# One sum per token for the norms, a block transposition on VectorE, and other partition halves in the first level of a triangular inverse

## The reference, cut to what matters

```python
def rmsnorm(x, g):
    y = xf * lax.rsqrt(jnp.mean(xf * xf, axis=-1, keepdims=True) + EPS)
    return (y * g.astype(jnp.float32)).astype(x.dtype)
```

```python
kb = k * beta[..., None]
Lmat = jnp.where(strict, jnp.einsum('bhnid,bhnjd->bhnij', kb, k) * decay, 0.0)
rhs = jnp.concatenate([v * beta[..., None], kb * jnp.exp(gc)[..., None]], axis=-1)
sol = lax.linalg.triangular_solve(eye + Lmat, rhs, left_side=True, lower=True, unit_diagonal=True)
```

## Time and profile before

| what | value |
|---|---|
| median of 3 runs | 1916.28 us (1915.13 to 1918.05) |
| the profiled execution, its own time | 1917.52 us |
| its span, first to last instruction | 1915.6 us |
| PE busy | 99% of the span |
| DVE, ACT, POOL busy | 62%, 41%, 16% |
| chain that ended last | PE 91%, DVE 5%, ACT 2%, issue 1%, POOL 1% |
| mean granted TensorE clock | 0.994 |

### The profile page before, as it was taken

How to read it: one execution, slowest core, us unless ns; L and a number is a source line. 1 busy time by engine, 2 the same in 40 slices (tenths; PEclk the granted TensorE clock), 3 DMA queues, 4 the chain that set the end, 5 groups by cost and what they waited for, 6 DMA issues and landing times.

```text
span 1915.6 us, 29959 instructions
## 1 busy us (share of the span) xinstructions
PE 1889.2 (99%) x10740; PEld 1539.3 (80%) x10740; DVE 1195.6 (62%) x1844; ACT 792.1 (41%) x1495; POOL 301.1 (16%) x222
## 2 busy tenths in 40 slices
PE   9999999999999999999999999999999999999997
PEld 7888878888888767777778888888887888888886
DVE  4997554333333777777745856737778568476474
ACT  4234443232233555555533423424547534243242
POOL 2532222111011200000111100101221211011012
PEclk9999999999999999999999999999999999999998
DMA  5232323232322112111112332232311123323231
GB/s 195 90 101 98 133 70 109 95 99 89 108 88 99 45 56 68 55 62 62 51 45 88 110 110 88 88 109 89 122 66 56 67 88 110 100 88 99 88 109 66
DMA packets 46946, 170.49 MB, mean 89 GB/s; under 512 B 5344, under 2 KB 5504, under 8 KB 46720
## 3 DMA queue, kind: packets, MB, share of 16 engines
q1 hardware_dynamic: 45648, 165.12, 26.0%
q10 hardware_dynamic: 1200, 3.95, 0.6%
HBM read 166.94 MB, written 2.11 MB: 88 GB/s over the span
## 4 chain that ended last, share of the span: by engine, by line
PE 91%; DVE 5%; ACT 2%; issue 1%; POOL 1%; DMA 0%; DVEq 0%; SPq 0%; POOLq 0%
PE ps L275 19%; PE ps L277 17%; PE ps L276 17%; PE ps L263 9%; PE ps L264 9%; PE ps L265 9%; PE ps L694 1%; PE ps L714 1%; PE ps L669 1%; PE ps L314 1%; DVE scr L1556 1%; DVE scr L1547 1%; DVE Y L1547 1%; PE ps L447 0%; PE ps L315 0%
## 5 line engine op out<-in xcount | busy, mean ns | idle before, releaser
L222 ACT ACTIVATE w_hi<-w_raw 128x1024 fp32r<-128x1024 f32 x304 | 316.9, 1050 | 269.7 <-PE ps L277 176.5
L227 DVE TENSOR_TENSOR w_lo<-w_raw,w_hi 128x1024 fp32r<-128x1024 f32 x255 | 344.4, 1354 | 124.3 <-ACT w_hi L222 123.6
L275 PE MATMUL ps<-A_hi,w_hi 128*128 128x512 f32 x896 | 367.0, 410 | 2.1 <-DVE Y L1046 1.1
L277 PE MATMUL ps<-A_hi,w_lo 128*128 128x512 f32 x896 | 350.6, 391 | 0.0
L276 PE MATMUL ps<-A_lo,w_hi 128*128 128x512 f32 x896 | 350.0, 391 | 0.0
L275 PE MATMUL ps<-B_hi,w_hi 128*128 128x512 f32 x688 | 271.3, 394 | 1.3 <-DVE B_lo L1083 0.9
L277 PE MATMUL ps<-B_hi,w_lo 128*128 128x512 f32 x688 | 268.0, 390 | 0.0
L276 PE MATMUL ps<-B_lo,w_hi 128*128 128x512 f32 x688 | 267.8, 389 | 0.0
L275 PEld LDWEIGHTS ps<-A_hi,w_hi 128*128 128x128 f32 x896 | 168.6, 188 | 39.1 <-issue 2.6
L277 PEld LDWEIGHTS ps<-A_hi,w_lo 128*128 128x128 f32 x896 | 168.6, 188 | 36.5
L276 PEld LDWEIGHTS ps<-A_lo,w_hi 128*128 128x128 f32 x896 | 169.0, 189 | 29.0
(11 more groups left out here) (296 smaller groups left out, 2611.7 us busy)
## 6 DMA issues: line engine op xcount, KB each, us to landing
w_raw<-d_ws SPq DMA_DIRECT2D x304, 512.0 KB, 3.5
X<-d_xT SPq DMA_DIRECT2D x4, 512.0 KB, 7.1
X<-d_xT ACTq DMA_DIRECT2D x1, 2048.0 KB, 8.1
d_out<-X SPq DMA_DIRECT2D x4, 512.0 KB, 2.6
scr<-gc_rows ACTq DMA_DIRECT2D x7, 256.0 KB, 3.2
cst<-d_cst SPq DMA_DIRECT2D x1, 800.0 KB, 11.6
par<-d_par SPq DMA_DIRECT2D x1, 344.5 KB, 3.1
scr<-d_pw SPq DMA_DIRECT2D x1, 256.0 KB, 12.7
```

The source lines that it names most:

```text
L222: nc.scalar.activation(w_hi[:, c], raw[:, c], ACT.Copy).then_inc(S(f"w_hi{s}"), 1)
L227: nc.vector.tensor_tensor(w_lo[:, c], raw[:, c], w_hi[:, c].bitcast(F32), ALU.subtract)\
L275: pe.matmul(ps[bank][:], w_hi[:, c], hi, start=k == 0, stop=False)
L277: last = pe.matmul(ps[bank][:], w_lo[:, c], hi, start=False, stop=k == total - 1)
```

## The change

It has three parts.

1. **The opening.** The sum of the squares moves from POOL to DVE and takes all eight tiles; PE takes one group of token sums. The first two slots of weights are split in halves of 512 columns, with a semaphore for each, and PE's order starts with the half that is there. ACT squares a pair of tiles one step later. `keep_warm` has 19 products in place of 22.
2. **The other token sums.** Except for post0, post1 and fin, POOL adds the last square too and PE takes one group of four matmuls. In `open_late` it stands after the third unit.
3. **The heads.** DVE transposes `TTC` in blocks of 32 x 32 (level 0 has nothing outside 2 x 2 blocks). The level-0 matrices of c = 2, 3 are written to the other half of the partitions, and level 1 becomes a crossed level like 2 to 5, with no transposition on PE and no copy on ACT. Six blocks run ahead of it in one piece.

```diff
@@ the opening, PE
-                if q < 3:
+                if q < 2:
+                    pe.wait_ge(S("early_hi"), count("early_hi", q + 1))
+                    pe.wait_ge(S("early_lo"), count("early_lo", q + 1))
+                    part_blocks(pe, open_bank(q, spare), q, pair, 0, 2 * q + 2, KT, wait)
+                elif q == 2:
                     open_segment(pe, r, q, pair, 0, 2 * q + 2, wait, spare)
-            sums_early(pe, tag, KT, 2)
-            sums_last(pe, tag, KT, 2, FIRST_SQ[KT - 1])
-            open_segment(pe, r, 3, pair, 0, KT - 2, wait, spare)
+            token_sums(pe, tag, KT, 2)
+            open_segment(pe, r, 3, pair, 0, KT - 4, wait, spare)
             pe.wait_ge(S("cst_in"), count("cst_in", 16))
             open_row(pe, tag)
-            open_segment(pe, r, 3, pair, KT - 2, KT, wait, spare)
+            open_segment(pe, r, 3, pair, KT - 4, KT, wait, spare)
...
@@ the opening, DVE in place of POOL
-        def first_sum_squares(pool):
-            pool.wait_ge(S("w_lo3"), count("w_lo3", 1))
-            for m in range(1, KT - 1):
...
+        def first_sum_squares(dve):
+
+            for m in range(1, KT):
+                dve.wait_ge(S("n0_sq"), count("n0_sq", m + 1))
                 if m > 1:
-                    pool.wait_ge(S("n0_ss"), count("n0_ss", m - 1))
-                nc.gpsimd.tensor_tensor(SS[:], FIRST_SQ[0] if m == 1 else SS[:], FIRST_SQ[m], ALU.add)\
+                    dve.wait_ge(S("n0_ss"), count("n0_ss", m - 1))
+                nc.vector.tensor_tensor(SS[:], FIRST_SQ[0] if m == 1 else SS[:], FIRST_SQ[m], ALU.add)\
                     .then_inc(S("n0_ss"), 1)
@@ the token sums
-            for m in range(1, n - 1):
+            for m in range(1, n - (tag in POST)):
                 pool.wait_ge(S(tag + "_sq"), count(tag + "_sq", m + 1))
...
         def token_sums(pe, tag, n, bank):
-            sums_early(pe, tag, n, bank)
-            sums_last(pe, tag, n, bank)
+
+            pe.wait_ge(S(tag + "_ss"), count(tag + "_ss", n - 1))
+            for c in range(NCH):
+                last = pe.matmul(ps[bank][:, c:c + 1], SS[:, c * P:(c + 1) * P], ones[:, 0:1],
+                                 start=c == 0, stop=c == NCH - 1)
+            last.then_inc(S(tag + "_sum"), 1)
@@ open_late
             for s in range(3):
                 open_segment(pe, r, s, pair, 0, KT - late, wait, spare)
-                if s == 1:
-                    sums_early(pe, tag, KT, 2)
-                elif s == 2:
-                    sums_last(pe, tag, KT, 2)
+            token_sums(pe, tag, KT, 2)
@@ delta_pe
-            dense(4, 3)
+            dense(6, 4)
             pe.wait_ge(S("zeros"), count("zeros", ZEROS))
-            for i in range(2):
-                pe.wait_ge(S("d_tt"), at("d_tt", i + 1))
-                for c in (2 * i, 2 * i + 1):
-                    last = transposed64(pe, ps[4 - i], TTC, c)
-                last.then_inc(S("d_ptr"), 1)
-            dense(2, 1)
...
@@ delta_dve
-                        v.tensor_tensor(x[half_], LAv[half_, 2 * i:2 * i + 2, 0, half_],
+                        v.tensor_tensor(x[half_of(b ^ i)], LAv[half_, 2 * i:2 * i + 2, 0, half_],
                                         twice(level(0))[half_], ALU.mult).then_inc(S("d_x"), 1)
                     dve.wait_ge(S("d_x"), at("d_x", 2 * i + 2))
                     v.tensor_tensor(two(pair64(TTC, i)), twice(ident64), x, ALU.subtract).then_inc(S("d_tt"), 1)
+                    dve.wait_ge(S("d_tt"), at("d_tt", i + 1))
+                    if i == 0:
+                        v.transpose(pair64(TC, 0), pair64(TTC, 0)).then_inc(S("d_t"), 1)
+                    else:
+                        for b in range(2):
+                            v.transpose(pair64(TC, 1)[half_of(b)], pair64(TTC, 1)[half_of(1 - b)])\
+                                .then_inc(S("d_t"), 1)
```

More of the change, by code:

```diff
@@ L387, in build, with early_half, squares @@
         FIRST_SQ = [tile(SG, 1 + m) for m in range(KT)]
+        def early_half(s, part):
+            return slice(s * 1024 + part * 512, s * 1024 + (part + 1) * 512)
         def first_norm_act(act):
+            def squares(*tiles):
+                for m in tiles:
+                    nc.scalar.activation(FIRST_SQ[m], tile(X, m), ACT.Square).then_inc(S("n0_sq"), 1)
             for q in range(SLOTS):
@@ L677, in delta_pe @@
             last.then_inc(S("d_trv"), 1)
[L678 removed]
+            dense(6, 4)
             pe.wait_ge(S("zeros"), count("zeros", ZEROS))
[L680 to L689 removed]
+            def crossed_level(l):
+                if l > 1:
+                    for i in range(2):
+                        pe.wait_ge(S("d_tt"), at("d_tt", 2 * (l - 1) + i + 1))
+                else:
+                    pe.wait_ge(S("d_t"), at("d_t", 3))
+                    pe.wait_ge(S("d_kvr"), at("d_kvr", 2 * NCH))
                 for n in range(2):
@@ L698, in crossed_level @@
                                 last.then_inc(S("d_px"), 1)
[L699 to L705, removed]
+                if l > 1:
+                    for n in range(2):
+                        for b in range(2):
+                            for i in range(2):
+                                last = pe.matmul(square64(ps[6 + i], n, b ^ i), square64(TC, 2 * i + n, b),
+                                                 ident64[64 * b:64 * b + 64, :], start=True, stop=True)
+                                if n and b:
+                                    last.then_inc(S("d_ttr"), 1)
                 fill(l, 0)
@@ L723, in delta_pe @@
                 for i in range(2):
[L724 to L729, removed]
-                    for c in (2 * i, 2 * i + 1):
[L731 to L738, removed]
+                    pe.wait_ge(S("d_tt"), at("d_tt", 2 * (l - 1) + i + 1))
+                    for c in (2 * i, 2 * i + 1):
+                        last = pe.matmul(square64(ps[4 + i], c % 2, 1), LAv[0:64, c, 0, 64:P],
+                                         square64(TC, c, 0), start=True, stop=True)
                     last.then_inc(S("d_px"), 1)
-                    if l > 1:
-                        for c in (2 * i, 2 * i + 1):
-                            last = transposed64(pe, ps[6 + i], TC, c)
-                        last.then_inc(S("d_ttr"), 1)
+                    for c in (2 * i, 2 * i + 1):
+                        last = transposed64(pe, ps[6 + i], TC, c)
+                    last.then_inc(S("d_ttr"), 1)
                 fill(l, 0)
@@ L746, in delta_pe @@
                     pe.wait_ge(S("d_x"), at("d_x", 2 * l + 3 + i))
-                    if l == 1:
-                        if i:
-                            pe.wait_ge(S("d_kvr"), at("d_kvr", 3 * NCH))
-                        pe.wait_ge(S("d_o1"), at("d_o1", 0))
-                    else:
-                        pe.wait_ge(S("d_ttc"), at("d_ttc", 8 + 2 * (i + 1)))
-                    for c in (2 * i, 2 * i + 1):
-                        if l == 1:
-                            for b in range(2):
-                                last = pe.matmul(columns(square64(ps[6 + i], c % 2, b), l, 0), square64(TTC, c, b),
-                                                 columns(square64(XB, c, b), l, 0), start=True, stop=True)
-                        else:
-                            last = pe.matmul(square64(ps[6 + i], c % 2, 0), square64(XB, 4 + c, 1),
-                                             diagonal(TTF, c, 1), start=True, stop=True)
+                    pe.wait_ge(S("d_ttc"), at("d_ttc", 8 + 2 * (i + 1)))
+                    for c in (2 * i, 2 * i + 1):
+                        last = pe.matmul(square64(ps[6 + i], c % 2, 0), square64(XB, 4 + c, 1),
+                                         diagonal(TTF, c, 1), start=True, stop=True)
                     last.then_inc(S("d_pt"), 1)
@@ L1835, in _ @@
             pe.wait_ge(S("const"), count("const", 2))
-            keep_warm(pe, 22)
+            keep_warm(pe, 19)
             def glu_round(i, first):
@@ L2087, in _ @@
                 v.tensor_scalar(half[:, at:at + n], par_range(name, n), 0.5, None, ALU.mult).then_inc(S("halved"), 1)
-            for m in range(KT):
-                x_loaded(dve, m)
-                norm_lo(dve, "n0", "mix_pre", pairA, m)
-                if m % 2:
-                    split_lo(dve, 0, m // 2)
+            first_low_parts(dve)
+            first_sum_squares(dve)
             token_mean(dve, "n0", 2, D)
```

53 lines of the change are left out of this document (37 added, 16 removed).

## The result

The changed kernel takes 1899.39 us in the median of four runs (1897.6 to 1902.05), the kernel before 1915.7 on the same chip (1914.38 to 1918.05). The ratio is 0.9916 with a 95% interval of 0.9900 to 0.9931: 16.3 us faster. The forecast was 1897.8, in a range of 1894.0 to 1904.0; the saving was put at 18.5.

What follows compares the result with a forecast made beforehand. PE was taken as the bound, busy 1889.2 of 1915.6 us. Gains of 5.2 (opening), 4.1 (token sums), 9.0 (heads) and 0.2 (na and head 0) sum to 18.5, from 1916.28 to 1897.8 us; range 1894.0 to 1904.0.

Steps and rivals of the forecast that it cites:

- The opening: Up to 37.32 us: PE starts earlier and doesn't wait at its token sums, round ends at 32.1; gain 5.2 us.
- the second price: Old opening, 29.5 to 33.1 us: behind an idle PE the clock is 0.53 and ten matmuls take 3.6 us.
- The token sums: Sums after the opening: 0.90 us saved each at nf0, kv, n_f1, 0.9 at n1, 0.5 at ln; gain 4.1.
- the port question: At n1: POOL's addition starts just ahead of DVE's split, which is held on the shared port and late by 1.0 us.
- The third rival: At n1 DVE's split goes first, POOL's addition ends at 286.4 and PE waits 0.9 us: 1898.7 us; chance 0.15.
- The heads: Heads 1 to 7: dropped transposition and crossed level 1 save PE 1.29 us a head, 9.0 in all.
- It fits by a hair: Level 1 in the heads: DVE's mask ends at 755.44 us, PE asks for it at 755.59.
- na and head 0 together: PE gains 0.9 us at na, but DVE sets head 0; gain 0.2, up to 1.1 if DVE's chain comes forward.
- So that wait only grows: Start of head 0: PE's wait of 1.21 us for `TTC` gets longer as PE gains 0.9 at na.
- the five rivals: Chances: dear transpositions 0.12, slower than before 0.02, port at n1 0.15, opening gives less 0.13, later stage takes it back 0.05.
- dear transpositions: In the heads: DVE's transpositions take more than 0.35 us each; at 0.6 the loss is 6.0, 1903.8 us; chance 0.12.

Runs made afterwards that it cites:

- the extra transpositions: The changed kernel with two more 64x128 transpositions on DVE in each head, ahead of level 1: 1903.4 us, ratio to before 0.9942.
- the sum on POOL: The changed kernel with the opening's sum of squares on POOL again, half slots and all else as changed: 1904.03 us, ratio to before 0.9942.
- the whole slots: The changed kernel with the first two slots of weights whole as before, the sum still on DVE: 1900.52 us, ratio to before 0.9925.

## Why the prediction was right, and where it was not

**The opening** was right in its steps: first block at 8.46 (8.4 forecast), sums at 25.06 (25.3), additions of 0.78 (0.74) done at 23.75 (24.2), no wait, upper clock, next round at 31.93 (32.1). The first of the seven additions starts at 18.29, where 19.0 was reckoned, and that makes up for their being a little longer. That the first block varies, from 8.27 to 9.23 over the executions with the half slots, was not in it, nor that the gain does: 4.7 to 5.5 where the sum is on DVE. The two don't go together in every execution: behind the block at 8.27 the gain was 5.1, behind that at 8.46 5.5. And the second price, the 3.6 us at 0.53, is one that the old opening doesn't pay in every execution: with the heads alone changed it didn't, and lay 1.9 ahead.

**The token sums** were right: 0.95 for 0.90 at the three late ones. At ln PE waits 0.25 for POOL. At n1 the port question went as taken: POOL first, the split held. POOL and DVE after:

```profile
277.98 1.33 POOL L466 TENSOR_TENSOR SS<-SS,SQ 128x512 f32<-128x512 f32 x1 [0.80 <-ACT SQ L452]
```

```profile
278.08 2.31 DVE L228 TENSOR_TENSOR w_lo<-w_raw,w_hi 128x1024 fp32r<-128x1024 f32 x1
280.58 0.16 DVE L494 TENSOR_SCALAR tok<-ps 128x4 f32<-128x4 f32 x1 [0.20 <-PE ps L488]
```

A split that takes 1.23 alone takes 2.31 and ends at 280.39, ahead of PE's request at 280.49. The third rival didn't come. POOL's addition ends at 279.31, and 1.23 behind that would be 280.54. The Trainium skill, "SBUF — State Buffer", section "SBUF: two separate sides", has the rule: of a DVE instruction with two inputs in SBUF and a GpSimd instruction that reads SBUF, the one that starts first holds the shared port pair for its whole instruction. The trace agrees to 0.15, with a price of 1.08 here.

**The heads.** 0.31 a transposition for the 0.3 taken; 1.3 a head for 1.29. The Trainium skill, "VectorE: DVE Perf Modes", section "The three transpose paths", gives 311 ns for 128 x 128 in bf16; for fp32 the trace has the same, 0.31 at 744.09. "It fits by a hair" was right in heads 2 to 6 and wrong in head 1, where DVE begins later (its first mask takes 0.70) and PE waits 0.37, and in head 7, where level 2 waits 0.55 for the update where it waited 0.42.

**The failed step** is na and head 0 together, "Gain 0.2". Its times up to the mask were right. Less the 6.75 by which PE is early ahead of na, level 1 was forecast at 667.65 and came at 667.72, the mask's end at 669.35 and came at 669.34. What followed was not: level 2 forecast at 670.65 came at 671.61. I wrote "So that wait only grows" and gave the longer wait no price beyond itself, though I had priced just that in the opening, where a wait of 1.07 was followed by 3.6 us at 0.53. The missing term is 1.0 in one execution and 4.0 in the other (1.7 and 4.7 less the 0.7 that head 0 costs with the wait filled). With the 0.4 of head 1 that is 1.4 in one execution and 4.4 in the other, on either side of the 2.2 by which the measured saving is short of 18.5. That the forecast came so near is luck in part: how long the clock stays down is no part of its sum, and the 19.9 between the two traces hold 2.7 that are low stretches of before.

None of the five rivals was this one. The nearest, dear transpositions, has the right engine and the wrong reason: they are not dear, but head 0 has no cover for them.

## What to carry to other kernels

Work that moves from PE to DVE costs nothing in the rounds where DVE has finished by the time PE asks; look for the one round where DVE sets the time already, since there the work moves onto the path. Where it makes PE stand still for longer, add what the clock can take afterwards, as a range, and consider a few idle products or a smaller edit for that round alone. When two profiled executions are compared, take out first the stretches that differ in granted clock only.

## What the hardware showed that I had not expected

- Behind PE's waits of 2.02 to 2.69 us in head 0 the lower clock came in all six executions that had one (the changed kernel twice, the heads alone, the extra transpositions, the sum on POOL, the whole slots). Behind waits of 1.15 to 1.27 at the same place it came in none of five (before, the opening alone, the sums alone, and the two with level 1 uncrossed there). Behind the wait of 1.07 to 1.08 at 27 us it came in two of three, behind that of 1.00 at post1's sums in ten of twelve, at fin's in seven of twelve. Yet in none of fourteen did it come behind a wait of 1.44 to 1.47 near 1430 us, nor behind one of 1.04 to 1.07 near 700 us. So the length of a wait alone doesn't tell; what else it takes, no run here separates.
- It stays down while PE is busy: 9.6 us at 0.50 with PE busy for 9.56 of them, on small matmuls and blocks alternately. The same wait cost 1.0 in one execution and 4.0 in another, 3.0 of the 4.75 us between the two. With head 0's wait, post1's and fin's filled or shortened, four runs lay within 0.52.
- A DVE transposition of 64x128 takes as long as one of 128x128 (0.32 and 0.31), and it may write to the other half of the partitions at that price.
